# 64 of 256 tokens look their experts up with gathers; the other 192 stay in dense expert products

## The chip, the core and the metric

The kernel runs on one core of a Trainium2 chip. The metric is device time in microseconds of the program, start to end; the median of three runs of the kernel before is 2287.76 us (2285.74 to 2288.77). A profiled execution gives the trace from which all rows below are read; its span, from the first instruction to the last, is 2284.1 us.

## The reference

Two blocks of a language model on 256 tokens of width 1024. The first block has two layers, each a mixer (retention, then differential attention) and a PEER layer, with layer norms. The second block has gated linear attention beside latent attention, cross attention and a feed-forward part. All is float32. The change concerns the two PEER layers:

```
q = (xc @ w_q).reshape(PEER_CHUNK, PEER_HEADS, 2, half)
sc = jnp.einsum('thpd,hpnd->thpn', q, subkeys)
s1, i1 = lax.top_k(sc[:, :, 0], PEER_TOPK)
s2, i2 = lax.top_k(sc[:, :, 1], PEER_TOPK)
...
top, pos = lax.top_k(cand, PEER_TOPK)
idx = jnp.take_along_axis(cidx, pos, axis=-1)        # 8 heads x 16 = 128 experts per token
gate = jax.nn.softmax(top, axis=-1)
u_e = jnp.take(u, idx, axis=0)
v_e = jnp.take(v, idx, axis=0)
act = jax.nn.gelu(jnp.einsum('ted,td->te', u_e, xc))
return jnp.einsum('te,ted->td', gate * act, v_e)
```

There are 16384 experts, each a row of 1024 numbers (4 KB) in u and one in v: 64 MB each, per layer.

## The kernel before

Each engine has its own hand-written program; semaphores tie them. Weights come as units of 128 x 1024 floats (512 KB): SyncE loads unit n into one of three raw buffers (`sp`, L3072) as soon as unit n-3 has been split. Splitting makes two rounded parts: ScalarE writes the high part (`hi_to`, L1373), VectorE or, for the units in `POOL_UNITS`, GpSimd the low part (raw minus high; L1967, L2973). TensorE then multiplies high by high, high by low and low by high parts, which together keep float32 precision at the rate of rounded operands. Rings of three places hold the parts (`hi`, `lo`, N_SPLIT); in the last units of a stage spare places are used too.

Each PEER layer is done densely, with stages per layer:
- peer_q: 16 units, the queries; then the scores against the keys (L889, plain float32 matmuls).
- peer_u, here called the first weights: 128 units, two per step c of 64. `feat_wide` (L633, L636) multiplies a unit by all 256 tokens: 8 matmuls with 512 columns (high and low parts of x) and 8 with 256. ScalarE copies one half of the sum (L1523), VectorE adds it (L2310), ScalarE applies the gelu (L1554, L1556).
- Beside its first half VectorE selects the experts (`topk`, L2200 to L2258), in short portions between its other work; at step 34 TensorE transposes the selection. From step 36 on the gates of four tokens at a time are spread over 128 x 128 places: one-hot rows by GpSimd (L2998), VectorE (L2292, L2294) and ScalarE (L1538, L1540), then 8 small matmuls (L915), then a product into the `experts` table (L2303).
- peer_v, the second weights: 128 units; experts' activations are the left operand, split into parts (L1410, L2033), two token tiles of 128 with 6 matmuls of 512 columns each (L705, L716).

The order of the work is fixed by these programs: `STEPS_AT` says at which half-step a group of four tokens is built and placed, `TOKENS` how many tokens already have their gates at a step.

## Time and profile before

| what | before |
|---|---|
| median of three runs | 2287.76 us |
| span of the profiled execution | 2284.1 us |
| TensorE busy | 2268.4 us (99%) |
| VectorE busy | 1699.0 us (74%) |
| ScalarE busy | 1324.8 us (58%) |
| GpSimd busy | 430.5 us (19%) |
| moved by transfers | 408.53 MB, mean 179 GB/s |

Busy times are those of the profiled execution. A matmul's duration overlaps that of its neighbours, so its pace is read from starts or from a group's busy time divided by its count. Line numbers are those of the kernel before.

### The profile page before, as it was taken

What the parts mean: (1) busy time and instruction counts of PE and PEld (TensorE: products, weight loads), DVE (VectorE), ACT (ScalarE), POOL (GpSimd) and SP (SyncE); (2) the same over time, 40 slices, a digit from 0 to 9 for tenths busy, and PEclk for the clock granted to TensorE, in tenths of its full rate; (3) what the DMA queues carried; (4) which work ended last, traced back from release to release, by engine and by line L of the source; (5) the groups of instructions that cost most, each with busy time, mean ns of one, the idle gap of its engine ahead of it and who ended that gap; (6) DMA issues with size and microseconds to landing.
All of it is one profiled execution on the core that took longest, in us unless ns stands there. A gap on an engine that the chain in (4) does not pass through costs nothing.

```text
span 2284.1 us, 33324 instructions
## 1 busy us (share of the span) xinstructions
PE 2268.4 (99%) x12380; PEld 1929.4 (84%) x12380; DVE 1699.0 (74%) x3098; ACT 1324.8 (58%) x2181; POOL 430.5 (19%) x355
## 2 busy tenths in 40 slices
PE   9999999999999999999999999999999999999999
PEld 9788888888888888887788888888888888877887
DVE  7567588999975555668758898997555666877885
ACT  3454555578765554646555558776555564666554
POOL 1000233178710000000013316872000000000000
PEclk9999999999999999999999999999999999999999
DMA  7455455544455655644455554445556575333555
GB/s 257 156 176 190 161 191 189 183 167 156 149 194 193 203 193 194 231 163 142 141 171 187 193 177 169 153 155 190 194 193 232 184 227 179 135 123 118 185 186 173
DMA packets 112096, 408.53 MB, mean 179 GB/s; under 512 B 12592, under 2 KB 12640, under 8 KB 111680
## 3 DMA queue, kind: packets, MB, share of 16 engines
q1 hardware_dynamic: 107712, 391.63, 50.4%
q0 software_dynamic: 3504, 13.47, 1.7%
q8 instruction: 100, 1.64, 0.3%
q10 hardware_dynamic: 720, 1.31, 0.2%
q14 instruction: 60, 0.49, 0.1%
HBM read 405.30 MB, written 1.05 MB: 178 GB/s over the span
## 4 chain that ended last, share of the span: by engine, by line
PE 87%; DVE 9%; ACT 2%; issue 1%; DMA 1%; POOL 0%; ACTq 0%; DVEq 0%
PE ps L716 24%; PE ps L633 21%; PE ps L705 12%; PE ps L636 11%; PE ps L672 3%; PE ps L669 3%; PE ps L676 3%; DVE lo L1967 3%; PE ps L915 2%; PE ps L768 1%; DVE big L1973 1%; ACT hi L1373 1%; DVE big L2303 1%; PE ps L889 1%; PE ps L616 1%
## 5 line engine op out<-in xcount | busy, mean ns | idle before, releaser
L1967 DVE TENSOR_TENSOR lo<-raw,hi 128x1024 fp32r<-128x1024 f32 (+1 forms) x627 | 765.4, 1224 | 366.1 <-ACT hi L1373 363.6
L1373 ACT ACTIVATE hi<-raw 128x1024 fp32r<-128x1024 f32 x677 | 714.3, 1057 | 479.7 <-PE ps L716 270.7
L633 PE MATMUL ps<-xs,hi 128*128 128x512 f32 x2560 | 650.8, 396 | 1.0 <-DVE big L2918 1.0
L633 PEld LDWEIGHTS ps<-xs,hi 128*128 128x128 f32 x2560 | 459.2, 189 | 83.6 <-DVE big L2918 1.1
L636 PEld LDWEIGHTS ps<-xs,lo 128*128 128x128 f32 x2560 | 349.0, 190 | 25.8
L636 PE MATMUL ps<-xs,lo 128*128 128x256 f32 x2560 | 356.3, 282 | 0.0
L2998 POOL TENSOR_SCALAR lnp<-iota,selT 128x128 f32<-128x128 f32 x256 | 278.1, 1097 | 167.0 <-DVE negT L2345 88.9
L705 PE MATMUL ps<-hi,lefts 128*128 128x512 f32 x986 | 304.0, 389 | 0.0
L716 PE MATMUL ps<-lo,lefts 128*128 128x512 f32 x986 | 303.7, 389 | 0.0
L716 PE MATMUL ps<-hi,lefts 128*128 128x512 f32 x986 | 303.6, 389 | 0.0
L716 PEld LDWEIGHTS ps<-hi,lefts 128*128 128x128 f32 x986 | 184.9, 188 | 38.7 <-DVE lefts L2033 0.2
L716 PEld LDWEIGHTS ps<-lo,lefts 128*128 128x128 f32 x986 | 185.0, 188 | 38.6 <-DVE lo L1967 0.2
L705 PEld LDWEIGHTS ps<-hi,lefts 128*128 128x128 f32 x986 | 184.6, 188 | 37.9
L2973 POOL TENSOR_TENSOR lo<-raw,hi 128x1024 fp32r<-128x1024 f32 x51 | 122.6, 2404 | 303.0 <-ACT hi L1373 297.2
L1523 ACT ACTIVATE halves<-ps 128x512 f32<-128x512 f32 x140 | 83.4, 596 | 139.1 <-PE ps L636 138.8
L2310 DVE TENSOR_TENSOR ps<-ps,halves 128x512 f32<-128x512 f32 x128 | 88.4, 691 | 44.0 <-ACT halves L1523 43.8
L2033 DVE TENSOR_TENSOR lefts<-big,lefts 128x256 fp32r<-128x256 f32 x276 | 115.2, 419 | 2.3 <-ACT lefts L1410 2.2
L1410 ACT ACTIVATE lefts<-big 128x256 fp32r<-128x256 f32 x276 | 110.7, 402 | 8.2 <-PE ps L716 8.0
L669 PE MATMUL ps<-hi,xs 128*128 128x512 f32 (+1 forms) x332 | 107.3, 404 | 1.9 <-ACT xs L1447 1.9
L672 PE MATMUL ps<-hi,xs 128*128 128x512 f32 (+1 forms) x332 | 103.6, 393 | 0.5 <-DVE xs L2092 0.4
L676 PE MATMUL ps<-lo,xs 128*128 128x512 f32 (+1 forms) x332 | 102.7, 390 | 0.1
L1379 ACT ACTIVATE big<-ps 128x512 f32<-128x512 f32 (+6 forms) x121 | 64.8, 547 | 63.6 <-PE ps L676 38.8
(370 smaller groups left out, 2505.8 us busy)
## 6 DMA issues: line engine op xcount, KB each, us to landing
raw<-in_peer_u SPq DMA_DIRECT2D x256, 512.0 KB, 3.2
raw<-in_peer_v SPq DMA_DIRECT2D x256, 512.0 KB, 4.2
raw<-in_ret_vg SPq DMA_DIRECT2D x32, 512.0 KB, 3.2
raw<-in_peer_q SPq DMA_DIRECT2D x24, 512.0 KB, 3.2
raw<-in_ffn_up SPq DMA_DIRECT2D x22, 512.0 KB, 3.3
raw<-in_ffn_down SPq DMA_DIRECT2D x22, 512.0 KB, 4.0
raw<-in_ffn_gate SPq DMA_DIRECT2D x18, 512.0 KB, 4.3
raw<-in_ret_qk SPq DMA_DIRECT2D x16, 512.0 KB, 4.6
```

Of the source, the lines that this page charges most:

```text
L633: e.matmul(out, uh[:, k, :], xs[:, k, :, :].rearrange("p h t -> p (h t)"), start=k == 0, stop=False)
L636: ins = e.matmul(out[:, 0:S], ul[:, k, :], xh[:, k, :], start=False, stop=k == 7)
L669: e.matmul(out, xh[:, 2 * s + i, cut], uh[:, i, :], start=s == 0 and i == 0, stop=False)
L672: e.matmul(out, xl[:, 2 * s + i, cut], uh[:, i, :], start=False, stop=False)
L676: ins = e.matmul(out, xh[:, 2 * s + i, cut], ul[:, i, :], start=False, stop=s == 3 and i == 1)
L705: e.matmul(us[2 * t + f].view, left_h, uh[:, f * 512:(f + 1) * 512], start=first, stop=False)
L716: ins = e.matmul(us[2 * t + f].view, a, b[:, f * 512:(f + 1) * 512], start=False, stop=last and second != weights_late)
L1373: e.activation(parts(i)[0][:, 0:w], raw[:, i % N_RAW, 0:w], ACT.Copy).then_inc(s_hi, 1)
L1967: e.tensor_tensor(ul[:, 0:w], raw[:, i % N_RAW, 0:w], uh[:, 0:w].bitcast(F32), ALU.subtract).then_inc(s_lo, 1)
L2033: e.tensor_tensor(left_l, lhs(k), left_h.bitcast(F32), ALU.subtract).then_inc(s_ll, 1)
L2973: e.tensor_tensor(ul, raw[:, n % N_RAW, :], uh.bitcast(F32), ALU.subtract).then_inc(s_lop, 1)
L2998: ins = e.tensor_scalar(Peer.oha[i % 2][:, t % 4, :], iota[:, :], selT[:, 0, t:t + 1], selT[:, 2, t:t + 1], ALU.is_equal, ALU.mult)
```

## The change

Tokens 0 to 63 (`LOOKED`) no longer take part in the dense products. For them GpSimd gathers rows of experts with indirect transfers: 128 rows of 4 KB each, 64 gathers from u and 64 from v per layer. A gather serves two experts for each of the 64 tokens, since the tokens stand twice in the 128 partitions. VectorE makes a dot product of each gathered row with its token (`look`, q below 64), and later adds each gathered row of v, times gate and gelu, to a sum. Four row buffers are used in turn.

The other 192 tokens (`DENSE`) go through peer_u with plain float32 matmuls, 8 per unit with 192 columns, on unsplit weights in six plain buffers that lie where the split parts lie otherwise. So no unit of peer_u is split. 48 groups of four tokens are spread instead of 64, over steps 17 to 62 (`SPREAD`); the transposes of the selection move from step 34 to 14 (`LISTED`), and the selection is done in larger portions.

In peer_v the left operand of tile 0 has 64 dense tokens; their high parts and their low parts stand side by side in 128 columns, so that one matmul covers both: 10 matmuls per unit instead of 12. At the end `fold` adds the two halves of those columns and the looked-up sums with four plain matmuls. GpSimd makes the low part of every third unit of peer_v from 3 to 96.

```diff
 MLA_UNITS = {0: 2, 2: 3, 3: 4, 5: 5, 7: 6}
-FREE = 84
+LOOKED = 64
+DENSE = S - LOOKED
+GROUPS = DENSE // 4
+N_PLAIN, N_ROWS = 6, 4
+YIELDS, LISTED, SPREAD, LOOKS = 15, 14, 17, 9
...
@@ -212,25 +217,27 @@
 def peer_schedule():
...
-    steps, at, turns = {}, 0, 0
-    tokens, chunk = [], None
+    steps, looks, tokens, gathers, at, q = {}, {}, [], [], 0, 0
     for c in range(64):
         for j in range(2):
-            if c >= 36:
-                turns += 1
-                n = 2 if turns % 4 == 0 else 1
-                steps[c, j] = list(range(at, min(at + n, 66)))
-                at += n
-                if 65 in steps[c, j]:
-                    chunk = c
-            else:
-                steps[c, j] = []
-        tokens.append(4 * max(0, min(at, 66) - 2))
-    assert chunk is not None
-    return steps, tokens, 2 * chunk
-STEPS_AT, TOKENS, EARLY_EXPERTS = peer_schedule()
+            n = 1 if c >= SPREAD and (2 * (c - SPREAD) + j) % 9 < 5 else 0
+            steps[c, j] = list(range(at, min(at + n, GROUPS + 2)))
+            at = min(at + n, GROUPS + 2)
+            gathers += [q + N_ROWS] * len(steps[c, j])
+            n = 1 if c >= LOOKS and (2 * (c - LOOKS) + j) % 5 < 3 and q < LOOK_PAIRS else 0
+            looks[c, j] = list(range(q, q + n))
+            q += n
+        tokens.append(4 * max(0, at - 2))
+    assert at == GROUPS + 2 and q == LOOK_PAIRS, (at, q)
+    for k in range(128):
+        n = 1 if k >= 3 and q < 2 * LOOK_PAIRS and (k - 3) % 9 < 5 else 0
+        looks[k] = list(range(q, q + n))
+        q += n
+    assert q == 2 * LOOK_PAIRS
+    return steps, looks, tokens, gathers
+STEPS_AT, LOOKS_AT, TOKENS, GATHERS = peer_schedule()
...
+        plain = nc.alloc_sbuf_tensor_at("plain", [128, N_PLAIN, UNIT], F32, offset=split_at)
...
-        POOL_UNITS = (*range(1, 27, 2), *range(35, 59, 2))
+        POOL_UNITS = tuple(range(3, 99, 3))
         pool_order = [0] + [n for l in range(2)
-                            for n in (W.first[f"peer_q{l}"] + 3, *(W.first[f"peer_u{l}"] + i for i in POOL_UNITS))]
+                            for n in (W.first[f"peer_q{l}"] + 3, *(W.first[f"peer_v{l}"] + i for i in POOL_UNITS))]
...
-                    n = W.first[f"peer_u{l}"] + 2 * c
-                    u = psum.claim_pair(("u", l, c), UPPER, (s_used, n + 2), None if TOKENS[c] else (s_gelu, 64 * l + c + 1))
-                    for before in u.before:
-                        e.wait_ge(*before)
+                    u = claim(("u", l, c), UPPER, (s_pused, 128 * l + 2 * c + 2),
+                              None if TOKENS[c] else (s_gelu, 64 * l + c + 1))
...
                     for j in range(2):
-                        feat_wide(n + j, u.view[:, j, :], X_PEER[l])
+                        m = 128 * l + 2 * c + j
+                        w = plain[:, m % N_PLAIN, :].rearrange("p (k n) -> p k n", k=8)
+                        e.wait_ge(*plain_landed(m))
+                        for k in range(8):
+                            ins = e.matmul(u.view[:, j * DENSE:(j + 1) * DENSE], w[:, k, :], Peer.xT[:, k, :],
+                                           start=k == 0, stop=k == 7)
...
                         if c == 0 and j == 0:
...
-                    if c == 34:
+                    if c == LISTED:
...
+                h1 = psum.claim_bank(("mixed", l, 1), 1)
...
+                def unit(k):
+                    (uh, ul), (left_h, left_l) = parts(n0 + k), left_parts(q0 + k)
+                    both, own_h, own_l = left_h[:, 0:128], left_h[:, 128:S], left_l[:, 128:S]
+                    e.wait_ge(s_hi, n0 + k + 1)
+                    e.wait_ge(s_lh, q0 + k + 1)
+                    for i, (left, w, t) in enumerate(((own_h, uh, 2), (own_l, uh, 2), (both, uh, 0), (both, ul, 0), (own_h, ul, 2))):
+                        if i == 1:
+                            e.wait_ge(s_ll, q0 + k + 1)
+                        if i == 3:
+                            e.wait_ge(*low(n0 + k))
+                        for f in range(2):
+                            ins = e.matmul(us[t + f].view, left, w[:, f * 512:(f + 1) * 512],
+                                           start=k == 0 and i in (0, 2), stop=False)
+                    return ins
...
+            def fold(l):
+                e.wait_ge(*looked(l, 2 * LOOK_PAIRS))
+                e.wait_ge(s_fold, l + 1)
+                for f in range(2):
+                    y = psum.claim_bank((f"peer_v{l}", f), 4 + f)
+                    e.wait_ge(*y.before)
+                    cut = slice(f * 512, (f + 1) * 512)
+                    e.matmul(y.view, Peer.fold[:, LOOKED:192], Peer.sums[:, cut], start=True, stop=False)
+                    e.wait_ge(*use["mixed", l, f].freed)
+                    e.matmul(y.view, Peer.fold[:, 0:128], Peer.halves[:, cut], start=False, stop=True).then_inc(y.filled[0], 1)
+            peer(0, 0, between=lambda j: xs_tile(X_DIFF, xk, normed_x(1), 0) if j == 5 else None)
...
+                        e.tensor_tensor(left_l[:, 128:S], src[:, 128 - n:DENSE], left_h[:, 128:S].bitcast(F32),
+                                        ALU.subtract).then_inc(s_ll, 1)
+                    else:
+                        e.tensor_tensor(left_l, src, left_h.bitcast(F32), ALU.subtract).then_inc(s_ll, 1)
                 return left
...
+                def look(q):
+                    rows = Peer.rows[(2 * LOOK_PAIRS * l + q) % N_ROWS]
+                    if q == 0:
+                        e.wait_ge(s_xrep, 32 * (l + 1))
+                    if q == LOOK_PAIRS:
+                        e.wait_ge(s_lgate, 32 * (l + 1))
+                        e.wait_ge(s_lgelu, l + 1)
+                        tt(Peer.weight, Peer.weight, Peer.gate, ALU.mult)
+                        me.wait()
+                        e.wait_ge(s_zero, l + 1)
+                    e.wait_ge(*rows_landed(l, q))
+                    if q < LOOK_PAIRS:
+                        e.tensor_tensor_reduce(rows, rows, Peer.copies, 1.0, 0.0, ALU.mult, ALU.add,
+                                               Peer.act[:, q:q + 1]).then_inc(s_looked, 1)
+                    else:
+                        e.wait_ge(*looked(l, q))
+                        w = Peer.weight[:, q - LOOK_PAIRS:q - LOOK_PAIRS + 1]
+                        e.scalar_tensor_tensor(out=Peer.sums, in0=rows, scalar=w, in1=Peer.sums, op0=ALU.mult,
...
                                 place(i - 2, c)
-                    if c == 32:
+                        for q in LOOKS_AT[c, j]:
+                            look(q)
...
+            def look_up(l, q):
+                table = A[f"peer_ur{l}"] if q < LOOK_PAIRS else A[f"peer_v{l}"].rearrange("n p d -> (n p) d")
+                m, i = 2 * LOOK_PAIRS * l + q, q % LOOK_PAIRS
+                if q >= N_ROWS:
+                    e.wait_ge(*looked(l, q - N_ROWS + 1))
+                e.indirect_dma_start(out=Peer.rows[m % N_ROWS], out_offset=None, in_=table,
+                                     in_offset=bass.IndirectOffsetOnAxis(ap=Peer.idx[:, i:i + 1], axis=0)
+                                     ).then_inc(s_row[m % N_ROWS], 16)
...
+                list_out(l)
+                q = 0
+                for q in range(N_ROWS + 2):
+                    look_up(l, q)
+                gates_out(l)
+                q += 1
+                for i in range(GROUPS):
+                    while q < GATHERS[i]:
+                        look_up(l, q)
+                        q += 1
                     build(l, i)
-                e.wait_ge(*use["u", l, 63].freed)
-                ln_load(l, 1)
+                while q < LOOK_PAIRS + N_ROWS:
+                    look_up(l, q)
+                    q += 1
+                make_fold(l)
+                for k in range(128):
+                    if k in POOL_UNITS:
+                        low_part(W.first[f"peer_v{l}"] + k)
+                    for q2 in LOOKS_AT[max(0, k - 2)]:
+                        if q2 + N_ROWS < 2 * LOOK_PAIRS:
+                            look_up(l, q2 + N_ROWS)
+                    if k == 8:
+                        ln_load(l, 1)
+                    if k == 62:
...
+            def plain_load(l, i):
+                m = 128 * l + i
+                if i < N_PLAIN:
+                    e.wait_ge(s_used, split_before[m] + 1)
+                else:
+                    e.wait_ge(*plain_used(l, i - N_PLAIN + 1))
+                e.dma_start(plain[:, m % N_PLAIN, :], A[f"peer_u{l}"][i]).then_inc(s_plain[m % N_PLAIN], 16)
+            n = 0
+            for l in range(2):
+                end = W.first[f"peer_q{l}"] + 16
+                for n in range(n, end):
+                    unit_load(n)
+                for i in range(128):
+                    plain_load(l, i)
+                    if i in (117, 120, 123):
+                        n += 1
+                        unit_load(n)
+                n += 1
```

The instructions of three places, in the order of the program of one engine. First TensorE, where the selection is transposed (`ident,big`: three times two squares of 128) and the units of peer_u stand around it; before:

```order
L633 MATMUL ps<-xs,hi 128x512 x8
L636 MATMUL ps<-xs,lo 128x256 x8
L768 MATMUL ps<-ident,big 128x128 x6
L633 MATMUL ps<-xs,hi 128x512 x8
L636 MATMUL ps<-xs,lo 128x256 x8
```

and of the change, from the second set of key scores on (`big` holds keys, queries and the plain x in turn):

```order
L990 MATMUL ps<-big,plain 128x192 x8
L950 MATMUL ps<-big 128x128 x16
L990 MATMUL ps<-big,plain 128x192 x232
L828 MATMUL ps<-ident,big 128x128 x6
L990 MATMUL ps<-big,plain 128x192 x48
L976 MATMUL ps<-lnp 128x128 x8
```

The transposes now stand behind 240/8 = 30 units of peer_u, where 70 stood before; each unit is one row of eight instead of two.

GpSimd from a layer's low part of peer_q on; before (`lo` is a low part, `lnp` one-hot rows):

```order
L2973 TENSOR_TENSOR query_weights_57<-raw,query_weights_57 128x1024
L2973 TENSOR_TENSOR lo<-raw,hi 128x1024 x25
L2998 TENSOR_SCALAR lnp<-iota,selT 128x128 x128
L2985 DMA lnp<-in_ln_g 128x1024
L2986 DMA lnp<-in_ln_b 128x1024
```

and of the change (`in_peer_ur` is u as rows of experts; the gather's target lies in `big`):

```order
L3214 DMA big<-x 64x1024 x2
L3220 DMA big<-big 64x64 x2
L3221 MEMSET big 128x1024
L3205 DMA big<-in_peer_ur,big 128x1024 x6
L3229 DMA big<-big 64x64 x2
L3205 DMA big<-in_peer_ur,big 128x1024 x8
L3194 TENSOR_SCALAR lnp<-iota,selT 128x128 x2
L3205 DMA big<-in_peer_ur,big 128x1024
```

Six gathers stand ahead of the gates (the 64x64 copies behind them), the rest among the one-hot rows; the low parts moved from peer_u to peer_v.

VectorE in peer_v, one unit after the other; before:

```order
L1967 TENSOR_TENSOR lo<-raw,hi 128x1024
L2033 TENSOR_TENSOR lefts<-big,lefts 128x256
L1967 TENSOR_TENSOR lo<-raw,hi 128x1024
L2033 TENSOR_TENSOR lefts<-big,lefts 128x256
L1967 TENSOR_TENSOR lo<-raw,hi 128x1024
```

and of the change (L2530 adds a gathered row of v to the sum):

```order
L2530 SCALAR_TENSOR_TENSOR big<-big 128x1024
L2115 TENSOR_TENSOR lo<-raw,hi 128x1024
L2184 TENSOR_TENSOR lefts<-big,lefts 128x64
L2185 TENSOR_TENSOR lefts<-big,lefts 128x128
L2530 SCALAR_TENSOR_TENSOR big<-big 128x1024
L2184 TENSOR_TENSOR lefts<-big,lefts 128x64
L2185 TENSOR_TENSOR lefts<-big,lefts 128x128
```

A left part is two operations instead of one, look-ups stand ahead of low parts, and the unit whose low part GpSimd makes has none here.

## Rows read from the trace of the kernel before

**Rows 1.** The page's first part: engine, busy us (share), instructions.

```profile
PE 2268.4 (99%) x12380; PEld 1929.4 (84%) x12380; DVE 1699.0 (74%) x3098; ACT 1324.8 (58%) x2181; POOL 430.5 (19%) x355
```

**Rows 2.** Windows of the stages: length, busy by engine, granted clock, transfers' share, GB/s.

```profile
257.30:654.50 397.20, 396.31 (x2601) 349.65 (x2600) 356.62 (x827) 266.39 (x483) 198.49 (x153) 1.00 0.50 170
654.50:1003.50 349.00, 349.00 (x1545) 289.08 (x1545) 210.69 (x273) 181.54 (x264) 2.74 (x5) 1.00 0.60 203
...
sum 1493.50, PE 1491.65 PEld 1278.08 DVE 1137.94 ACT 899.16 POOL 406.00; mean PE 372.91 PEld 319.52 DVE 284.48 ACT 224.79 POOL 101.50
```

**Rows 3.** The chain of waits: start us, us, engine, line, count.

```profile
260.30 3.57 PE ps L889 x32
...
266.67 1.84 PE ps L633 x8
269.47 1.84 PE ps L633 x8
...
1969.96 5.16 PE ps L1136 x16
```

**Rows 4.** Timeline of TensorE in peer_v's last units: start us, us, instructions.

```profile
995.84 0.61 PE L705 MATMUL ps<-tail_weights,tail_left 128*128 128x512 f32 x2
...
997.20 0.61 PE L705 MATMUL ps<-tail_weights,tail_left 128*128 128x512 f32 x2
```

**Rows 5.** Groups of TensorE, 466 to 652 us: count, busy us, mean ns, idle.

```profile
L915 PE MATMUL ps<-lnp 128*128 128x128 f16 x512 | 39.4, 220 | 0.7 <-DVE lnp L2294 0.6
```

**Rows 6.** Timeline of VectorE: the selection's first and last instruction.

```profile
264.54 0.18 DVE L2215 CAST big<-iota 128x16 bf16<-128x16 f32 x1 [4.13 <-ACT big L1379]
...
462.41 0.19 DVE L2345 TENSOR_SCALAR negT<-selT 128x32 f32<-128x32 f32 x1
```

**Rows 7.** Groups of VectorE, 264.4 to 463 us.

```profile
L1967 DVE TENSOR_TENSOR lo<-raw,hi 128x1024 fp32r<-128x1024 f32 x47 | 57.8, 1229 | 6.7 <-ACT hi L1373 6.4
...
L2310 DVE TENSOR_TENSOR ps<-ps,halves 128x512 f32<-128x512 f32 x35 | 24.3, 694 | 18.6 <-ACT halves L1523 18.5
...
L2329 DVE TENSOR_TENSOR big<-big,sm 128x128 f32<-128x128 f32 x2 | 0.6, 292 | 0.1
```

**Rows 8.** Line 1579: the table load ahead of the exponentials, min/median/max ns.

```profile
L1579 ACT ACT_TABLE_LOAD  x2: 1283/1283/1283, 451.3 to 1369.5; - x2
```

**Rows 9.** Groups of VectorE, 466 to 652 us.

```profile
L1967 DVE TENSOR_TENSOR lo<-raw,hi 128x1024 fp32r<-128x1024 f32 x55 | 67.6, 1228 | 4.4 <-ACT hi L1373 3.8
L2294 DVE TENSOR_TENSOR lnp<-iota,selT 128x512 f16<-128x512 f32 x64 | 45.7, 714 | 0.0
L2303 DVE SCALAR_TENSOR_TENSOR big<-ps,big 128x296 f32<-128x296 f32 (+24 forms) x64 | 35.5, 555 | 2.0 <-ACT big L1546 1.6
L2292 DVE TENSOR_SCALAR lnp<-iota,selT 128x128 f32<-128x128 f32 x64 | 22.0, 343 | 0.2
```

**Rows 10.** The page's groups of GpSimd.

```profile
L2998 POOL TENSOR_SCALAR lnp<-iota,selT 128x128 f32<-128x128 f32 x256 | 278.1, 1097 | 167.0 <-DVE negT L2345 88.9
...
L2973 POOL TENSOR_TENSOR lo<-raw,hi 128x1024 fp32r<-128x1024 f32 x51 | 122.6, 2404 | 303.0 <-ACT hi L1373 297.2
```

**Rows 11.** Line 2985: a transfer issued by GpSimd, ns on its queue (min/median/max).

```profile
L2985 POOL DMA_DIRECT2D lnp<-in_ln_g x4: 534/594/607, 15.3 to 1577.6; - x4
```

**Rows 12.** Windows: five microseconds near the start.

```profile
20.00:25.00 5.00, 5.00 (x42) 4.86 (x42) 3.44 (x6) 1.06 (x1) 0.00 (x0) 1.00 1.03 417
```

**Rows 13.** Transfers in 40 slices of 660 to 980 us, in GB/s.

```profile
GB/s 341 217 199 190 187 187 193 189 186 198 187 200 236 217 196 196 197 198 198 193 188 196 187 188 188 196 190 194 195 194 196 196 198 197 222 253 257 264 222 245
```

**Rows 14.** Issues of transfers: count, KB, median us to landing; page, then 945 to 985 us.

```profile
raw<-in_peer_v SPq DMA_DIRECT2D x256, 512.0 KB, 4.2
...
raw<-in_peer_v SPq DMA_DIRECT2D x16, 512.0 KB, 3.4
```

**Rows 15.** Groups of VectorE, 652 to 985 us.

```profile
L2033 DVE TENSOR_TENSOR lefts<-big,lefts 128x256 fp32r<-128x256 f32 x122 | 51.0, 419 | 1.7 <-ACT lefts L1410 1.6
```

**Rows 16.** The page's group of high parts on ScalarE.

```profile
L1373 ACT ACTIVATE hi<-raw 128x1024 fp32r<-128x1024 f32 x677 | 714.3, 1057 | 479.7 <-PE ps L716 270.7
```

More of the change, by code:

```diff
@@ L436, in build @@
             sel = [several(R, 3, 8, 16), several(R, 3, 8, 16)]
-            keys = region(big, 14848)(2, UNIT)
+            listed = R(128, dt=U32)
+            keys = region(big, 12288)(2, UNIT)
+            R = region(big, 24576)
+            sums, copies = R(UNIT), R(UNIT)
+            rows = several(R, N_ROWS, UNIT)
+            idx, act, weight, gate = R(64, dt=U32), R(64), R(64), R(64)
+            xT = R(8, DENSE)
+            halves = region(big, 31744)(UNIT)
+            fold = selT.rearrange("p s t -> p (s t)")[:, 0:192]
             oha = [lnp[:, s, 0:512].rearrange("p (u n) -> p u n", u=4) for s in range(2)]
@@ L591, in build @@
         L.settle()
+        in_ring = [[n for n in sorted(W.ring) if W.ring[n] == r] for r in range(N_SPLIT)]
+        split_before = {}
+        for l in range(2):
+            end = W.first[f"peer_q{l}"] + 16
+            for i in range(N_PLAIN):
+                m = 128 * l + i
+                split_before[m] = max(n for n in in_ring[m % N_PLAIN % N_SPLIT] if n < end)
+            for r in range(N_SPLIT):
+                n = min(n for n in in_ring[r] if n >= end)
+                m = max(m for m in range(128 * l, 128 * l + 128) if m % N_PLAIN % N_SPLIT == r)
+                W.after[n] = (*W.after.get(n, ()), (s_pused, m + 1))
         def pe(e):
@@ L2259, in topk @@
                                     ALU.subtract).then_inc(s_sel, 1)
+                    if t == 0:
+                        first, second = (a.rearrange("p h k -> p (h k)") for a in Peer.sel[0][0:2])
+                        e.scalar_tensor_tensor(out=Peer.listed, in0=first, scalar=128.0, in1=second, op0=ALU.mult,
+                                               op1=ALU.add).then_inc(s_idx, 1)
                     yield
@@ L3066, in sp, with unit_load @@
         def sp(e):
-            for n, src in enumerate(W.src):
+            def unit_load(n):
                 if n in (1, 2):
```

276 lines of the change are left out of this document (194 added, 82 removed).

## Prediction

> **What bounds the kernel now.** The page comes first: TensorE is busy for 99% of the span [rows 1]. The stretches by stage [rows 2] then say where: the first layer's first-weights stage (units of peer_u) lasts 397.2 us and its second-weights stage (peer_v) 349.0 us, the second layer's two are alike, and in the four together the matmuls leave 1.9 us free, at a granted clock of 1.00. They are 1493.5 of 2284.1 us, and nothing outside them is rewritten. The chain of waits shows the pace of one peer_u unit: 2.80 us from one group of eight to the next [rows 3]. In peer_v half a unit starts every 1.36 us, so a unit takes 2.72 us and one 512-column matmul 0.227 us [rows 4]. VectorE has the only other chain of note: the selection of experts, from 264.54 to 462.41 us [rows 6], woven between low parts and sums of halves [rows 7].
>
> **The first-weights stage: matmuls.** A unit was 8 wide and 8 narrow matmuls on rounded parts, 2.80 us. It becomes 8 plain matmuls with 192 columns. That shape is not in the trace. Plain matmuls on 128 columns take 3.57/32 = 0.112 us and on 384 columns 5.16/16 = 0.323 us, each with its own load of weights [rows 3]; on the line between them 192 columns cost 0.165 us, so a unit costs 1.32 us. The 48 groups of spread matmuls instead of 64 cost 39.4/512 x 8 = 0.62 us each [rows 5]. TensorE's work falls from 397 to 128 x 1.32 + 48 x 0.62 + 3.6 = 202 us. All splitting of peer_u and all sums of halves go. What is late next has two pieces.
>
> **First piece, until the selection ends.** TensorE stops in front of the transposes of the selection after 30 units (before: 70), because list position 14 takes the place of 34. The order shows it. VectorE has the selection to itself now. Its own time for it is the stretch of 198.6 us less 57.8 + 6.7 us of low parts and 24.3 + 18.6 us of sums, with their waits: 91 us [rows 7]. It gets six look-ups, priced like the nearest row with the same size and two inputs, 1.23 us [rows 9], so 7.4 us, and the exponentials' table load of 1.28 us with two activations and semaphores is no longer covered: 2.5 us [rows 8]. The selection starts about 6 us into the stage (7.2 us now, less 1.5 us of the shorter unit). Sum: 6 + 91 + 7.4 + 2.5 = 107 us, and TensorE moves on at about 105 us. Its 30 units are done by 30 x 1.32 + 3.6 = 43 us, so it stands for 62 us per layer, and so does the transfer of weights, since only six plain buffers exist.
>
> **Second piece, from there.** 98 units are left, 92 of them not yet loaded, and 62 gathers: GpSimd's order has six ahead of the gates, then 58 of the first table and four ahead for the second. VectorE meets the seventh look-up before it copies the transposed selection, and so waits there for a gather that begins only with the gates: some 5 us, of which the plain units that need no selection hide most. Per nine half-steps there are 9 units, 5.4 look-ups and 5 groups placed:
> - TensorE: 9 x 1.32 + 5 x 0.62 = 15.0 us.
> - VectorE: 5 x (0.71 + 0.34 + 0.56) + 4.5 x 0.42 + 5.4 x 1.23 = 16.6 us [rows 9]; the 0.42 us, for the product with the gelu, is the row of 256 columns [rows 15].
> - GpSimd: 10 x 1.10 = 11.0 us of one-hot rows [rows 10], and 5.4 gathers. No gather is in the trace. A direct transfer on this queue holds it for 0.6 us, its longest instruction for 2.4 us [rows 10, 11]; I take 1.2 us, nearer to the direct one, for its 128 indices: 17.5 us.
> - Transfers: 14.4 x 0.524 MB. The fastest stretch moves 417 GB/s with the engines full [rows 12], so 1.26 us each: 18.1 us, the longest. At the 341 GB/s of the best slice in a peer_v stage [rows 13] it is 22.1 us.
>
> By transfers alone the rest is 154 x 1.26 = 194 us; by VectorE alone some 173 us. Four engines within a fifth of each other don't overlap fully, and the start costs some us: I take 208 us, between 194 and 250. Stage: 105 + 208 = 313 us, a gain of 84 per layer.
>
> The Trainium skill, DMA: Bandwidth & Descriptors, section Where 436 GB/s comes from, says that transfers from HBM are bound by the HBM side at about 358 GB/s per core. By that page the 154 transfers would take 225 us, an estimate, and the total some 60 us more than I forecast. The row of 417 GB/s speaks against it for this core alone.
>
> **The second-weights stage.** A unit has 10 matmuls instead of 12, because one matmul serves both the high and the low parts of tile 0's 64 dense tokens: 2.27 us. For 128 units that would be 291 instead of 349 us. VectorE per unit with GpSimd's help: two thirds of a low part (0.82), two left parts (0.29 for 128 columns, about 0.22 for 64: 0.51, instead of 0.42 for one [rows 7, 15]), and 5/9 of a look-up (0.68): 2.0 us; from unit 99 on, without GpSimd, 2.4 us. Transfers: 14/9 x 1.26 = 1.96 us. What is late is the ring of three raw buffers. At the end of the stage now, where spare places for the parts free it from TensorE, a turn of it is landing 3.4 [rows 14], high part 1.06 [rows 16] and low part 1.23 us, 5.7 us; the loads run at 253 to 264 GB/s [rows 13], 2.03 us each and 6.1 us for three, so hand-overs take 0.4 us. Now every third unit's low part is GpSimd's, 2.40 us [rows 10], always in the same place of the ring: 3.4 + 1.06 + 2.40 + 0.4 = 7.3 us for three units, 2.4 us each; 2.7 at a landing of 4.2 us, and 3.1 with a whole gather (1.26 us) ahead of every load besides. I take 2.6 us, so the ring replaces TensorE as the bound: 96 x 2.6 + 20 x 2.45 + 12 x 2.27 = 326 us, and 8 us for the hand-over (the split places are the plain buffers, so high parts wait for the last plain units), the fold's four plain matmuls (1.7 us) and tile 0's transposes. Stage: 334 us, a gain of 15.5, between 300 and 365 us.
>
> **Smaller edits.** Copying the plain x out of PSUM adds four operations to the norm's chain, 1 us per layer. The list, gate and x copies, the zeroed sums and the fold matrix lie beside the selection or between gathers. Earlier constants and the raw loads of the next stage lie beside peer_v; nothing.
>
> **Sum.** 2 x (84 + 15.5 - 1) = 197 us. The profiled span of 2284.1 us becomes 2087 us; the median of the runs is 3.7 us above the span, so 2091 us.
>
> **Rivals.**
> 1. Both stages run at their engines' pace: 299 and 300 us, that is 2 x (98 + 49 - 1) = 292 us, 1996 us. For it: six plain buffers and four row buffers run well ahead. Against: the ring sum. Chance 0.15.
> 2. The ring or the looks are worse: peer_v at 360 us, peer_u at 345 us: 2 x (52 - 11 - 1) = 80 us, 2208 us. For it: loads of peer_v landed in 4.2 us at 203 GB/s already [rows 2, 14] and now share with gathers. Chance 0.17.
> 3. The other side: gathers cost GpSimd much more. Both stages queue low parts or one-hot rows behind them. peer_u takes 105 + 94/9 x (11.0 + 5.4 g), so it breaks even at g = 3.1 us; peer_v is bound by (3 x 2.40 + 5 g)/9 per unit. Together the change loses from g = 3.3 us on; at 4 us peer_u is 446 and peer_v 386 us, and the time 2460 us. For it: no indirect transfer is in the trace, and VectorE is always at work beside it. Against: direct ones keep to 0.53 to 0.61 us beside a busy VectorE [rows 11]. Chance 0.10.
> 4. TensorE falls to its lower level, 1.2 GHz, and stays there: it stands for 62 us and then has gaps, while now every stage shows the granted clock of 1.00 [rows 2] without an idle stretch. A unit would take 2.64 and a spread 1.24 us: peer_u 105 + 98 x 2.64 + 48 x 1.24 = 423 us, with peer_v unchanged 2 x (-26 + 15) is 22 us lost, 2310 us. Against: at half rate it has no gaps and would rise again. Chance 0.03.
> 5. The plain matmul doesn't get cheaper at 192 columns, twice the line's value: 105 + 98 x 2.64 + 30 = 394 us, 2253 us. Against: two shapes that agree. Chance 0.03.
>
> On rival 3, the Trainium skill, SBUF — State Buffer, section SBUF: two separate sides, says that a GpSimd transfer whose descriptors are locked out by VectorE takes about 3100 instead of 620 ns. At 3.1 us, an estimate by that page, peer_u gains nothing and peer_v 15, so 2259 us. The trace shows no direct transfer held that long; whether an indirect one is, no row can tell.
>
> **How the numbers follow.** The forecast has 0.52 with 2040 to 2150 us as its own range; rivals 0.15, 0.17, 0.10, 0.03 and 0.03. Eight in ten lie from 2005 to 2195 us. A measurement tells 0.2%, about 4.6 us. Slower: rivals 3 and 4, 0.13, less the milder part of 3, 0.11. Within 0.2%: 0.02. Faster: 0.87.
>
> **What would show it.** In peer_u: eight plain matmuls in 1.32 us; TensorE idle some 60 us behind VectorE's gates; then idle times that end with landings of plain, at 380 GB/s or more. Gathers on GpSimd near 1.2 us. In peer_v: units at 2.6 us with high parts waiting for landings, every third low part 2.40 us on GpSimd. If TensorE waits there for VectorE's look-ups instead, the ring was not the bound; if its waits end with GpSimd's one-hot rows in peer_u, the gather's price was wrong.

## The result, and the profile after

The changed kernel takes 2348.97 us (median of four runs, 2346.93 to 2357.09) against 2287.26 us of the kernel before: a ratio of 1.0275, 95% interval [1.0258, 1.0292]. It is slower by 62 us. I had predicted 2091 us, within 2005 to 2195 us, and gave "slower" 0.11: wrong in sign.

The stages' windows of the profile after; columns as in [rows 2], the same four stages in the same order, then the last row their sum:

```profile
259.40:645.20 385.80, 364.83 (x2473) 360.88 (x2471) 247.82 (x762) 93.48 (x261) 183.93 (x171) 0.97 0.78 269
645.20:1029.00 383.80, 331.12 (x1290) 242.56 (x1289) 311.82 (x430) 173.26 (x263) 172.28 (x97) 0.96 0.78 267
1202.40:1596.00 393.60, 366.97 (x2473) 362.65 (x2471) 248.17 (x762) 93.80 (x262) 183.33 (x171) 0.97 0.76 266
1596.00:1985.10 389.10, 332.48 (x1305) 243.51 (x1306) 312.59 (x466) 178.27 (x284) 183.22 (x103) 0.97 0.78 266
sum 1552.30, PE 1395.41 PEld 1209.61 DVE 1120.39 ACT 538.81 POOL 722.77; mean PE 348.85 PEld 302.40 DVE 280.10 ACT 134.70 POOL 180.69
```

The first-weights stage of layer 0 goes from 397.2 to 385.8 us (of layer 1 from 397.3 to 393.6 us), with TensorE still busy for 364.8 us of it; the second-weights stage goes from 349.0 to 383.8 us (from 350.0 to 389.1 us), with TensorE not busy for 53 us of layer 0's where it had no gap. The four stages together are 58.8 us longer than in [rows 2] (1552.3 less 1493.5), of 63.4 us between the spans.

**First weights.** The page's group of plain matmuls (count, busy us, mean ns, idle), then two pieces of the chain of waits between 330 and 420 us (start us, us, what):

```profile
L990 PE MATMUL ps<-big,plain 128*128 128x192 f32 x4096 | 692.9, 329 | 4.1 <-DMA plain<-in_peer_u 4.1
```

```profile
363.66 17.50 PE ps L990 x96
381.62 2.65 PE ps L990 x16
```

The stage has 256 units of 8 plain matmuls, 2048 in all. The trace has 4096 of them. Each plain float32 matmul stands there as two records, and a unit is "x16" and 2.65 us, not 1.32. Only one wait of TensorE is left over from my forecast, from the waits of TensorE between 262 and 640 us (waiter, what ended it, us, times, longest):

```profile
PE ps L828 <- DVE big L2493: 20.9, 1, 20.9
```

**Second weights.** The groups of VectorE from 660 to 940 us, which are the second-weight units of layer 0 without their start and end:

```profile
L2530 DVE SCALAR_TENSOR_TENSOR big<-big 128x1024 f32<-128x1024 f32 x55 | 99.0, 1799 | 0.0
L2115 DVE TENSOR_TENSOR lo<-raw,hi 128x1024 fp32r<-128x1024 f32 x65 | 83.0, 1276 | 27.3 <-ACT hi L1512 27.2
L2184 DVE TENSOR_TENSOR lefts<-big,lefts 128x64 fp32r<-128x64 f32 x95 | 51.7, 545 | 15.5 <-ACT lefts L1551 15.4
L2185 DVE TENSOR_TENSOR lefts<-big,lefts 128x128 fp32r<-128x128 f32 x95 | 26.6, 280 | 0.0
```

95 units in 280 us are 2.95 us a unit (2.6 forecast). VectorE's operations add up to 260.3/95 = 2.74 us of each (2.0 forecast, added up in the same way; neighbouring records overlap at their ends, and the time in which VectorE is busy is 237.2 us, 2.50 us a unit). The counts are as planned, but the operations are longer: its look-up (L2530) has a mean of 1.80 us and the small left part (L2184) one of 0.54 us. The timeline of VectorE and GpSimd shows where the mean comes from:

```profile
803.47 4.06 DVE L2530 SCALAR_TENSOR_TENSOR big<-big 128x1024 f32<-128x1024 f32 x1
...
804.04 2.39 POOL L3168 TENSOR_TENSOR lo<-raw,hi 128x1024 fp32r<-128x1024 f32 x1
...
809.69 0.22 DVE L2184 TENSOR_TENSOR lefts<-big,lefts 128x64 fp32r<-128x64 f32 x1
...
812.75 2.40 POOL L3168 TENSOR_TENSOR lo<-raw,hi 128x1024 fp32r<-128x1024 f32 x1 [3.99 <-ACT hi L1512]
...
812.95 2.27 DVE L2184 TENSOR_TENSOR lefts<-big,lefts 128x64 fp32r<-128x64 f32 x1
```

A left part that takes 0.22 us alone takes 2.27 us when it starts just after GpSimd's low part, and ends with it. A look-up of 1.27 us takes 4.06 us, although it started 0.57 us before the low part. And the chain of waits from 660 to 700 us shows landings of raw far over the 4.2 us of [rows 14]:

```profile
667.73 6.51 DMA raw<-in_peer_v
...
676.61 8.16 DMA raw<-in_peer_v
...
696.21 4.29 DMA raw<-in_peer_v
```

Both are candidates for the lost time, with GpSimd's 2.4 us in one place of the ring as a third. The experiments separate them.

### The profile page after: what moved, and what is told of

Same layout as the page of the kernel before. It is cut to its first block, busy times and chain, and to the rows that moved or that the text cites. A ratio compares the mean times of both kernels' runs of the same rounds, so it can differ in the third digit from the quotient of the medians.

```text
span 2347.5 us, 31540 instructions
## 1 busy us (share of the span) xinstructions
PE 2174.3 (93%) x11628; PEld 1860.8 (79%) x11628; DVE 1683.1 (72%) x3296; ACT 961.9 (41%) x1737; POOL 748.6 (32%) x579
## 4 chain that ended last, share of the span: by engine, by line
PE 51%; DVE 26%; DMA 13%; issue 4%; ACT 4%; POOL 1%; ACTq 0%; DVEq 0%; POOLq 0%
PE ps L990 22%; DMA raw<-in_peer_v 11%; DVE big L2530 7%; DVE lo L2115 4%; PE ps L776 4%; PE ps L732 3%; PE ps L729 3%; PE ps L693 3%; PE ps L736 3%; ACT hi L1512 2%; DVE big L2359 2%; PE ps L976 2%; PE ps L765 2%; DVE big L2121 2%; DVE big L2355 2%
## 5 line engine op out<-in xcount | busy, mean ns | idle before, releaser
L990 PE MATMUL ps<-big,plain 128*128 128x192 f32 x4096 | 692.9, 329 | 4.1 <-DMA plain<-in_peer_u 4.1
L990 PEld LDWEIGHTS ps<-big,plain 128*128 128x128 f32 x4096 | 668.7, 191 | 4.3 <-issue 4.3
L1512 ACT ACTIVATE hi<-raw 128x1024 fp32r<-128x1024 f32 x421 | 443.9, 1058 | 536.4 <-DMA raw<-in_peer_v 325.7
L2115 DVE TENSOR_TENSOR lo<-raw,hi 128x1024 fp32r<-128x1024 f32 (+1 forms) x357 | 444.0, 1249 | 188.5 <-ACT hi L1512 187.2
L1046 PE MATMUL ps<-hi,lefts 128*128 128x512 f32 x1320 | 381.4, 412 | 80.5 <-DVE lefts L2185 63.3
L3205 POOL DMA_INDIRECT big<-in_peer_v,big x128 | 190.9, 1491 | 209.8 <-DVE big L2530 173.2
L2530 DVE SCALAR_TENSOR_TENSOR big<-big 128x1024 f32<-128x1024 f32 x128 | 217.5, 1699 | 0.1
L2525 DVE CUSTOM_DVE_ANT_0 big<-big 128x1024 f32<-128x1024 f32 x128 | 156.9, 1237 | 14.9 <-DMA big<-in_peer_ur,big 14.9
L2184 DVE TENSOR_TENSOR lefts<-big,lefts 128x64 fp32r<-128x64 f32 x244 | 112.6, 462 | 40.1 <-ACT lefts L1551 40.0
L693 PE MATMUL ps<-xs,hi 128*128 128x512 f32 x512 | 128.7, 393 | 1.0 <-DVE big L3111 1.0
L693 PEld LDWEIGHTS ps<-xs,hi 128*128 128x128 f32 x512 | 92.2, 189 | 17.8 <-DVE big L3111 1.1
```

Of the source, the lines that this page charges most:

```text
L693: e.matmul(out, uh[:, k, :], xs[:, k, :, :].rearrange("p h t -> p (h t)"), start=k == 0, stop=False)
L990: ins = e.matmul(u.view[:, j * DENSE:(j + 1) * DENSE], w[:, k, :], Peer.xT[:, k, :], start=k == 0, stop=k == 7)
L1046: ins = e.matmul(us[t + f].view, left, w[:, f * 512:(f + 1) * 512], start=k == 0 and i in (0, 2), stop=False)
L1512: e.activation(parts(i)[0][:, 0:w], raw[:, i % N_RAW, 0:w], ACT.Copy).then_inc(s_hi, 1)
L2115: e.tensor_tensor(ul[:, 0:w], raw[:, i % N_RAW, 0:w], uh[:, 0:w].bitcast(F32), ALU.subtract).then_inc(s_lo, 1)
L2530: e.scalar_tensor_tensor(out=Peer.sums, in0=rows, scalar=w, in1=Peer.sums, op0=ALU.mult, op1=ALU.add).then_inc(s_looked, 1)
```

## The experiments on the second weights

The theories: A, the gathers' bytes lengthen the landings, and the ring of three feels each; B, VectorE and GpSimd hold each other up; C, VectorE simply has too much to do; D (named when the fifth run below was made), GpSimd's slow low parts cost time because the ring and TensorE wait for them. Changes are against the changed kernel; ratios are to the kernel before.

**1. VectorE makes all low parts.**

```diff
-        POOL_UNITS = tuple(range(3, 99, 3))
+        POOL_UNITS = ()
```

> The changed kernel with GpSimd's low parts of the second weights given back to VectorE (VectorE makes all 128 a layer; the look-ups stay). The second weights' stage took 384 and 389 us at 3.0 us a unit where 2.27 us of TensorE's matmuls were expected. Theory B (VectorE and GpSimd hold each other up: operations of VectorE that take 1.27 us are seen at 4.1 us beside a GpSimd low part of 2.4 us): VectorE's own work is about 1.06 + 0.5 + 0.7 = 2.3 us a unit, so the stage falls to about 2.4 us a unit, 310 us, and the kernel to about 2200 us. Theory A (the look-ups' rows share the transfers, and the ring of three raw places feels each landing): GpSimd's low parts are innocent, the time stays within 1% of 2349 us. Theory C (VectorE has too much to do): a third more low parts on it make it slower, about 0.35 us a unit, 2440 us.

Measured 2305.12 us, 1.0084 [1.0067, 1.0101]: 44 us less. More work on VectorE made the kernel faster, which is against C as the whole cause, and the time lies outside A's 1% too. VectorE's groups from 660 to 940 us:

```profile
L2115 DVE TENSOR_TENSOR lo<-raw,hi 128x1024 fp32r<-128x1024 f32 x99 | 120.8, 1220 | 53.0 <-ACT hi L1512 52.8
L2530 DVE SCALAR_TENSOR_TENSOR big<-big 128x1024 f32<-128x1024 f32 x59 | 75.3, 1276 | 0.0
...
L2184 DVE TENSOR_TENSOR lefts<-big,lefts 128x64 fp32r<-128x64 f32 x103 | 22.3, 216 | 0.0
```

Every kind of operation is back at its own price (1276 and 216 ns), but the gain is 44 us and not the 150 that B promised: the unit is still 2.75 us, and VectorE now waits 53 us for high parts, which wait for landings.

**2. Small gathers.**

```diff
+                n = UNIT if q < LOOK_PAIRS else 64
+                if n < UNIT:
+                    table = table.rearrange("r (b d) -> (r b) d", d=n)
-                e.indirect_dma_start(out=Peer.rows[m % N_ROWS], out_offset=None, in_=table,
+                e.indirect_dma_start(out=Peer.rows[m % N_ROWS][:, 0:n], out_offset=None, in_=table,
```

> The changed kernel, but each gather of the second weights brings 64 columns instead of 1024, so 32 KB instead of 512 KB; the number of gathers, the waits and VectorE's operations are the same (the looked-up tokens' sums are then not the reference's). Theory A (shared transfers and the ring of three): traffic falls from 1.5 x 512 KB to 512 KB a unit, the stage goes from 384 to about 300 to 320 us, the kernel to about 2200 us. Theory B (VectorE and GpSimd hold each other up): unchanged, 2320 to 2350 us.

Measured 2310.51 us, 1.0097 [1.008, 1.0114]: 38 us less. The bytes cost something: more than B alone allowed, and far less than A alone needed.

**3. A small operation on each gathered pair.**

```diff
-                        e.scalar_tensor_tensor(out=Peer.sums, in0=rows, scalar=w, in1=Peer.sums, ...
+                        e.scalar_tensor_tensor(out=Peer.sums[:, 0:64], in0=rows[:, 0:64], scalar=w, in1=Peer.sums[:, 0:64], ...
```

> The changed kernel, but VectorE's operation on each gathered pair in the second weights' stage works on 64 of 1024 columns; gathers, bytes and waits are the same (the looked-up tokens' sums are then not the reference's). It takes about 0.7 us a unit off VectorE and the long meetings with GpSimd's low part at that place. Theory B or C (VectorE): the stage falls to 320 to 340 us, the kernel to about 2230 us. Theory A (transfers): 2330 to 2350 us.

Measured 2316.95 us, 1.0128 [1.0111, 1.0145]: 32 us less, and again no theory's number.

**4. No look-ups of second weights.** The edit of 3, `look_up` returns before the gather for q from 64 on, and VectorE doesn't wait for rows there.

> The changed kernel without the gathers of the second weights, and with VectorE's operation on them cut to 64 columns (the looked-up tokens' sums are then not the reference's); GpSimd's low parts and TensorE's ten matmuls a unit stay. It shows what the ten matmuls alone are worth. If nothing but the look-ups holds the stage up, it goes at TensorE's pace of 2.27 us a unit, 291 us and a few more, and the kernel is at about 2170 us. If GpSimd's low parts in one ring place hold it up even without look-ups, the stage stays at 330 us or more, the kernel at 2240 us or more.

Measured 2244.62 us, 0.9816 [0.9799, 0.9832]. From its first to its last full unit the stage takes 307.4 us, 2.52 us a unit, against 359.2. The time is that of the second expectation, a stage held up by GpSimd's low parts even without look-ups. They meet the small left part there, which has a mean of 0.80 us (VectorE, 660 to 940 us):

```profile
L2184 DVE TENSOR_TENSOR lefts<-big,lefts 128x64 fp32r<-128x64 f32 x113 | 90.1, 797 | 47.4 <-ACT lefts L1551 47.4
```

Where nothing is late, TensorE goes at the forecast pace (timeline, starts 2.27 us apart):

```profile
800.28 1.07 PE L1046 MATMUL ps<-lo,lefts 128*128 128x512 f32 x4
...
802.55 1.07 PE L1046 MATMUL ps<-lo,lefts 128*128 128x512 f32 x4
...
804.82 1.07 PE L1046 MATMUL ps<-lo,lefts 128*128 128x512 f32 x4
```

**5. and 6. Small gathers, or no look-ups, with all low parts by VectorE.** Edits 1 with 2, and 1 with 4.

> The changed kernel with both edits: VectorE makes all low parts of the second weights, and each of their gathers brings 64 columns instead of 1024 (the looked-up tokens' sums are then not the reference's). Alone they measured 2305 us (44 us gained) and 2310 us (38 us). If the two are separate causes that add (GpSimd's 2.4 us in one place of the ring, and the gathers' share of the transfers), this gives about 2267 us. If both only shorten the same turn of the ring, and VectorE with its 2.3 to 2.5 us a unit is next, it gives 2290 to 2305 us. If the two only mattered through GpSimd meeting VectorE, about 2300 us as well.

> The changed kernel with no gathers of the second weights, VectorE's operation on them cut to 64 columns (the looked-up tokens' sums are then not the reference's), and all low parts made by VectorE. With GpSimd's low parts kept this measured 2245 us, 2.52 us a unit. If those low parts, each 2.4 us in the same place of the ring of three, are what is left over TensorE's 2.27 us, the units now go at 2.27 to 2.35 us and the kernel is at 2195 to 2210 us. If the landing itself holds the units (about 2.0 us a load at 256 GB/s), nothing changes: 2240 us.

Measured 2257.72 us, 0.9869 [0.9852, 0.9885], and 2213.20 us, 0.9668 [0.9652, 0.9685]. The first is 91 us under the changed kernel, 9 us more than the two edits gained alone (82 us), where 2267 us was expected if they add. The second is 136 us under it, 12 us less than the two alone (148 us), and 3 us above the expected 2195 to 2210 us. So the causes add only roughly. Without the looks the unit is 2.39 us.

**7. The small operation, with all low parts by VectorE.** Edits 1 with 3.

> The changed kernel with all low parts of the second weights by VectorE (2305 us alone) and VectorE's operation on each gathered pair of second weights cut to 64 of 1024 columns, 0.28 instead of 1.28 us (the looked-up tokens' sums are then not the reference's); the gathers bring all their bytes. 128 such operations lose 1.0 us each. With small gathers instead the time was 2258 us, with neither 2213 us. If VectorE's time counts in full on the turn of the ring, wherever the bytes are, about 45 us come off as they did from 2258 to 2213: 2260 us. If with whole gathers the landing ends last at nearly every unit, VectorE's second is hidden behind it: 2285 to 2300 us.

Measured 2280.66 us, 0.9976 [0.9966, 0.9985], between the two expectations. The square of medians is then full:

| second-weight look-ups | GpSimd makes 32 low parts | VectorE makes all | difference |
|---|---|---|---|
| whole | 2349.0 | 2305.1 | 43.9 |
| small gathers | 2310.5 | 2257.7 | 52.8 |
| small operation | 2317.0 | 2280.7 | 36.3 |
| neither | 2244.6 | 2213.2 | 31.4 |

GpSimd's low parts cost 31 to 53 us in every row. In the right column the bytes are worth 47.4 us, the operation 24.5 us, and both 91.9 us: 20 us more than their sum. That each hides part of the other behind the ring is a reading of this number; no run shows it apart.

**8. GpSimd busy, but in nobody's way in the ring.** It tells B from D.

```diff
-        POOL_UNITS = tuple(range(3, 99, 3))
+        POOL_UNITS = ()
...
+                e.wait_ge(*looked(l, LOOK_PAIRS))
...
-                    if k in POOL_UNITS:
-                        low_part(W.first[f"peer_v{l}"] + k)
+                    if k in range(3, 99, 3):
+                        e.wait_ge(s_hi, W.first[f"peer_v{l}"] + k + 1)
+                        me.wait()
+                        me.did(e.tensor_tensor(Peer.copies, Peer.copies, Peer.copies, ALU.subtract))
```

> The changed kernel with VectorE making all low parts of the second weights (2305 us alone), but GpSimd does a subtraction of the same size at the same 32 units on a place of its own that nobody reads and nobody waits for. GpSimd is then busy as in the changed kernel, but not in the ring of three raw places. Theory B (GpSimd's operation holds VectorE's up, 4.1 us seen instead of 1.27): each of the 64 still costs VectorE 1 to 2.8 us, the time goes back to 2340 us or more. Theory D (GpSimd's 2.4 us cost because TensorE's unit and one raw place wait for them): nothing changes, 2305 us, within 0.3%.

Measured 2362.28 us, 1.0334 [1.0315, 1.0352]: 57 us more than without the idle subtraction, and more than the changed kernel. Nobody waits for its result. VectorE's groups from 660 to 940 us:

```profile
L2530 DVE SCALAR_TENSOR_TENSOR big<-big 128x1024 f32<-128x1024 f32 x54 | 100.4, 1859 | 0.0
L2184 DVE TENSOR_TENSOR lefts<-big,lefts 128x64 fp32r<-128x64 f32 x93 | 36.9, 397 | 0.0
```

The look-ups are back at 1.86 us with no idle time ahead of them, so they don't wait for the gathers that the subtraction puts off. So B is shown: GpSimd operations that nobody waits for lengthen VectorE's, and cost 57 us where giving the low parts back to VectorE had gained 44 us. D isn't needed for those 44 us, but isn't ruled out as a smaller part: TensorE's waits that end with GpSimd's low part are 26.5 us in the two layers of the changed kernel. What the delayed gathers add elsewhere wasn't measured apart.

## The experiment on the first weights

**9. Half the matmuls.**

```diff
-                        for k in range(8):
+                        for k in range(4):
                             ins = e.matmul(u.view[:, j * DENSE:(j + 1) * DENSE], w[:, k, :], Peer.xT[:, k, :],
-                                           start=k == 0, stop=k == 7)
+                                           start=k == 0, stop=k == 3)
```

> The changed kernel with four of the eight plain matmuls of every unit of the first weights (the dense tokens' first products are then half sums, not the reference's). The trace has two records a plain matmul, so eight take 2.61 us and TensorE is busy through the stage of 386 us. If TensorE is what bounds it and my other terms (VectorE 16.6, GpSimd 17.5, transfers 18.1 us for nine units) are about right, the units go at 2.0 to 2.1 us once the experts are listed, TensorE waits longer for the selection, and the stage is 300 to 320 us: 66 to 86 us less a layer, the kernel at about 2200 us. If something else also stands near the limit (VectorE and GpSimd holding each other up, transfers with gathers among them), the stage is 340 us or more and the kernel at 2260 us or more.

Measured 2226.28 us, 0.9751 [0.9718, 0.9784], 123 us less than the changed kernel. This kernel has the unit price that I had forecast by mistake, and its stage takes 327.5 us (forecast: 313; expected before this run: 300 to 320). TensorE's waits from 262 to 590 us, then two windows:

```profile
PE ps L828 <- DVE big L2493: 58.0, 1, 58.0
PE ps L976 <- issue: 34.5, 26, 2.4
PE ps L976 <- POOL lnp L3194: 11.0, 2, 9.1
PE ps L990 <- DMA plain<-in_peer_u: 6.5, 7, 3.0
```

```profile
420.00:460.00 40.00, 32.75 (x241) 30.83 (x240) 29.06 (x63) 17.86 (x53) 34.50 (x32) 0.96 1.01 398
...
500.00:540.00 40.00, 29.85 (x224) 27.59 (x224) 31.57 (x64) 15.15 (x48) 37.34 (x33) 1.00 1.01 392
```

It waits 58.0 us for the selection (62 forecast), and then the transfers are full at 392 to 398 GB/s with GpSimd busy for 34 to 37 of 40 us. The rate is near the 417 GB/s of [rows 12] that the sum used, and above the one behind the 225 us that the prediction sets beside it. With this price the forecast's first-weights part comes out 14.5 us short, inside the range that it gave. Its sign to look for came only in part: the waits that end with landings of plain are 6.5 us, and 34.5 us stand ahead of the spread matmuls (L976) with no releaser that the profile shows. What held those isn't shown.

## Two versions that keep the computation

In the first-weights stage VectorE is busy for 248 of 386 us, and the selection, for which TensorE waits, has six look-ups of 1.15 us woven into its last stretch. So all low parts go to VectorE, and looks move into that stage.

**10. Four looks in five units, from unit 18.** The gelu of the looked-up products, its wait and the later looks follow; the rest of the looks is spread over the second weights.

```diff
-            n = 1 if c >= LOOKS and (2 * (c - LOOKS) + j) % 5 < 3 and q < LOOK_PAIRS else 0
+            n = 1 if c >= LOOKS and (2 * (c - LOOKS) + j) % 5 < 4 else 0
...
-        n = 1 if k >= 3 and q < 2 * LOOK_PAIRS and (k - 3) % 9 < 5 else 0
+        n = min(2 * LOOK_PAIRS, first + (2 * LOOK_PAIRS - first) * max(0, k - 2) // 114) - q
```

> The same computation as the changed kernel, with the looks in another place: during the first weights' stage four looks in five units instead of three, so the 64 of the first weights end earlier and 22 of the 64 of the second weights are made there, and only 42 in the second weights' stage; VectorE makes all low parts of the second weights. The first weights' stage has TensorE busy and VectorE free 40% of it, at 300 GB/s. If it stays TensorE's, it remains at 386 us, and the second stage, with a third of the looks gone, goes from 2.75 to about 2.6 us a unit: 2270 us. If the transfers or VectorE give way in the first stage (337 GB/s wanted with the gathers), it grows by 10 us or more a layer and the time is 2290 to 2310 us.

Measured 2280.03 us (2272.11 to 2292.3), 0.9967 [0.995, 0.9985], between the two expectations. The first stage grew to 393 us, the second goes at 2.59 us a unit.

**11. and 12. The first look after the listing (`LOOKS` 14 instead of 9), at four in five and at one in each unit.**

> The same computation as the changed kernel: all low parts of the second weights by VectorE, and four looks in five first-weight units, but the first look only after the experts are listed (unit 28 instead of 18), so none of them stands inside VectorE's selection, for which TensorE waits 20.9 us in the changed kernel (six looks of 1.15 us in its last stretch) and 23.1 us with four looks in five from unit 18. If the looks lengthen the selection, TensorE's wait falls to about 14 us, the first stage to about 384 us; 16 second-weight looks are made in the first stage and 48 stay: 2265 to 2275 us. If they only filled gaps of the selection, the wait stays at 21 us and the time at 2280 to 2290 us.

> As the run before, with a look in every first-weight unit once the experts are listed, so that 31 of the 64 second-weight looks are made in the first stage and 33 stay. The first stage then wants about 375 GB/s at TensorE's pace of 2.61 us; with half its matmuls it moved 388 to 398 GB/s. If transfers, GpSimd (about 36 of 40 us busy) and VectorE hold, its stage stays at 384 us and the second stage falls to about 2.5 us a unit: 2245 to 2255 us. If one of them gives way, the first stage grows to 400 us and the time is 2275 us or more.

Measured 2271.81 us, 0.9935 [0.9922, 0.9948], and 2274.94 us, 0.9957 [0.9941, 0.9973]. TensorE's longest wait, in the first and in the second of them:

```profile
PE ps L834 <- DVE big L2499: 14.2, 1, 14.2
```

```profile
PE ps L982 <- issue: 15.6, 13, 2.2
PE ps L834 <- DVE big L2499: 14.1, 1, 14.1
```

Six looks fewer in the selection are 6.7 us less of waiting, and the first of the two runs is where it was expected if the looks lengthen the selection. At one look a unit the second stage falls from 2.72 to 2.55 us a unit but the first one grows from 379 to 397 us, where TensorE's spread groups now wait. The first of the two computes what the changed kernel computes, in 77 us less, and is 0.65% faster than the kernel before.

## Why the prediction was wrong, point by point

- **What bounds the kernel**: right. All but 4.6 us of the difference between the spans lies in the four stages.
- **The plain matmul, the larger of the two steps that failed.** I divided 3.57 us by 32 and 5.16 us by 16 [rows 3] as if the counts of the chain were instructions. The code of the key scores (`key_scores`, two halves of x by eight keys) has 16 matmuls where the chain says x32. So the plain price was 0.223 us at 128 columns, and at 192 it measures 2.65/8 = 0.331 us instead of 0.165; a unit went from 2.80 to 2.65 us and not to 1.32. Of the gain of 84 us a layer 11.4 came in layer 0 and 3.7 in layer 1, so this step is 153 of the 258 us between forecast and result. Rival 5 had this mechanism and 394 us for the stage (385.8 measured), with a chance of 0.03, argued away with "two shapes that agree": both had the same error. Its check was at hand, in the count of the loop; the order of the program ahead of the prediction has the key scores as x16 too. The Trainium skill, FP8 and Floating Point Precision, section TensorE Precision Notes, says that a true float32 product takes four passes through the array. By that page a unit needs 8 x 192 x 4 columns at 2.4 GHz, 2.56 us, an estimate; the trace agrees within 4%, with 2.65 us at a granted clock of 1.00. I hadn't weighed that rule.
- **Selection**: right. The transposes start 102.6 us into the stage (105 forecast). TensorE stood only 20.9 us because its own units now fill that time; with half of them it stood 58.0 us.
- **Second piece**: covered by TensorE in the changed kernel; in experiment 9 the stage is 14.5 us longer than forecast, and what its waits end with is in part open. The gather's price was fair: medians of 1.00 us in the first weights, 1.68 us in the second (1.2 assumed, 3.3 needed for rival 3).
- **Second weights, the other step that failed.** TensorE's 2.27 us was right. The ring's 2.6 us was not: 2.95. The sum took VectorE at 2.0 us a unit and let it work beside GpSimd at no cost; its operations add up to 2.74 us. In place of the forecast gain of 15.5 us a layer came a loss of 34.8 and 39.1 us, 105 of the 258 us. About 31 us of the excess in 280 us stand at the small left part (95 x 0.33), 29 us at the look-up (55 x 0.52). The landings of 4.2 us, and at most one gather ahead of each load, were exceeded in single turns (6.5 and 8.2 us). Rival 2 named this side, at 360 us, and laid it to the transfers; it is 383.8 us.
- **The sign** took both steps. With the first alone the kernel would be faster by the prediction's own numbers (2253 us, rival 5). With the second alone it is faster too: experiment 9 has the forecast's price for a unit of first weights and the second-weights stage as it came, and takes 2226 us.
- **Rival 4, the clock**: it fell, and rose again. While TensorE stood for the selection the granted clock was 0.50 (350 to 360 us, the lower level, 1.2 GHz), in the 10 us in which it started again 0.63, and 1.00 in the next. The 96 records after the wait took 17.5 us where six units at full pace take 15.9. So it cost some 2 us in that place.
- **What I could have seen**: the trace before has such meetings. The clearest, VectorE's row first and GpSimd's behind it, is of operations with two SBUF inputs each (the first row holds two records):

```profile
309.32 3.36 DVE L1973 TENSOR_TENSOR big<-big 128x512 f32<-128x512 f32 x2
309.81 2.46 POOL L2973 TENSOR_TENSOR lo<-raw,hi 128x1024 fp32r<-128x1024 f32 x1 [3.18 <-ACT hi L1373]
```

The same two on VectorE, as min/median/max ns with first and last start:

```profile
L1973 DVE TENSOR_TENSOR big<-big x2: 693/1665/2637, 309.3 to 310.0; 128x512 f32<-128x512 f32 x1, 128x384 f32<-128x384 f32 x1
```

The 512 columns took 0.69 us; the 384 columns after them, begun beside the low part, took 2.64 us. In the changed kernel, where GpSimd makes no low parts in this stage, the same 384 columns take 0.56 us. Elsewhere VectorE's work beside GpSimd's low parts mostly read PSUM or had one input, so their means in [rows 7] show nothing. The Trainium skill, SBUF — State Buffer, section Who interferes with whom, states the rule: an instruction of VectorE with two SBUF inputs contends with one of GpSimd that reads SBUF. The trace agrees in both places (0.22 to 2.27 us; 0.56 to 2.64 us). The same section lets the order of issue decide who blocks, and the starts in the trace don't bear that out. In layer 0 of the changed kernel eight look-ups that began 0.57 to 0.60 us before a low part took 4.06 to 4.12 us, more than both operations one after the other (1.27 + 2.40 us). Four that began as early kept their 1.27 us, and the low part took 2.9 us. What decides between them isn't shown.

- **Sum**: the range held neither the result nor any mixture of rivals 2 and 5, which is what came. I had priced them as alternatives; together they are 2 x (3 - 11 - 1), 18 us slower, by the prediction's own numbers. The result is 62 us slower: the second-weights stages are 24 and 29 us longer than even rival 2 had them, and the first-weights stages 9 us shorter in all than rival 5 had them.

## What to carry to other kernels

Before dividing a duration by a count, check the count against the loop that issues it. Price an operation of VectorE by what GpSimd does beside it: here, where both had two operands in SBUF, work handed to GpSimd cost 31 to 53 us more than it saved. And ask of two rivals what they give together.

## What the runs showed that was not expected

- A GpSimd subtraction of 128 x 1024 whose result nobody needs, 32 times a layer, costs 57 us, about 0.9 us each, with what the gathers that it puts off may add.
- GpSimd's side is lengthened too: the same subtraction took 1.89 us at least, 2.93 us in the median and 5.06 us at most in experiment 8. That VectorE's work beside it does this was read from the trace, not tested apart:

```profile
L3268 POOL TENSOR_TENSOR big<-big x64: 1892/2930/5064, 654.6 to 1900.6; 128x1024 f32<-128x1024 f32 x64
```
- The square of experiments: of the 104 us that second-weight look-ups cost, removing the bytes alone gives 38 and the operation alone 32.
